# Gather buffers in borrowed memory, two expert steps behind every one-hot build

## The chip, the cores and the metric

The kernel runs on one core of one Trainium2 chip. The metric is the device time of one execution in microseconds.

## The reference

It is one inference step of a two-layer encoder over T = 576 frames (512 of a prompt and 64 of a running stream) of width 1024. Layer 0 mixes with a chunked gMLP, layer 1 with windowed attention. What matters here is the second half of each layer, a mixture of 16384 single-neuron experts:

```python
q = (xb @ w_q).reshape(blk, PEER_HEADS, 2, D_HALF)
sc = jnp.einsum('thpd,hpnd->thpn', q, sub_keys)
top_s, top_i = lax.top_k(sc, PEER_TOPK)                 # 8 heads, 2 halves, 16 of 128 keys
...
best_s, sel = lax.top_k(cand_s.reshape(...), PEER_TOPK)  # 16 of the 256 pairs
gate = jax.nn.softmax(best_s, axis=-1)
act = jax.nn.gelu(jnp.einsum('thkd,td->thk', exp_u[idx], xb))
return jnp.einsum('thk,thkd->td', gate * act, exp_v[idx])
```

Each frame picks 8 × 16 = 128 experts, each with a row of u and a row of v (2 × 1024 floats, 8 KB together).

## The kernel before

The frames are in two groups. Group d (256 frames, chunks 0 and 1) computes its experts densely on TensorE. Group g (320 frames, chunks 2, 3 and 4) gathers the rows that it needs.

**Dense part, per layer.** It goes over NPAIR = 64 pairs of expert columns. For each pair:

- SyncE loads 1 MB of u into `U[i % 2]` and 1 MB of v into `V[i % 2]`. The U load of pair i waits until the scores of pair i − 2 are done.
- TensorE computes `expert_scores(i)` (line 706) into bank i % 2, and ScalarE's `gelu(i)` (line 1059) writes it into a ring `gr` of RING = 16 entries.
- VectorE's `gate_product(i)` (line 1568) multiplies the ring entry by the gates in `Wr` and gives `a`.
- TensorE computes `expert_sums(i)` (line 719), which adds a × V.

The gates reach `Wr` through NBLD = 64 builds. VectorE's `one_hot(m)` (lines 1546 to 1557) makes one-hot tiles in two buffers, TensorE's `build(m)` (line 693) multiplies them, and ScalarE's `to_w(m)` (line 1051) copies the product out. one_hot(m) waits for build(m − 2). The gate product of pair 0 needs builds 0 to 15.

Each engine has its order written out by hand. On TensorE scores 0 to 6 come first (among the last selections); then, in what the text calls the hot stage, LEAD = 17 builds with scores 7 to 15 behind every second one; then a loop of sums(i), build(i + 17), score(i + 16); and from pair 48 on, sums alone.

**Gathered part, per layer.** It has NSTEP = 320 steps. In each, 128 partitions fetch one expert row of 8 KB: GpSimd issues an indirect DMA (`gather`, line 1259) into one of SLOTS = 6 slots, step s into slot s % 6, four of them in `gata` and two in `gatb`. VectorE forms a dot product with the frame (`dot_x`, line 1577), ScalarE a weight from it (lines 1065 and 1067), and VectorE adds weight × v row to `acc` (`axpy`, line 1585). `gathered(l, s)` is the dot of step s followed by the accumulation of step s − 1, and the gather into a slot waits for the accumulation that read it last (`ax_done`).

The table `AT` sets steps at places ahead of the pair loop: behind the adds of the output projection (`add`), the key searches (`top`), the selections (`sel`), attention units (`att`, layer 1), and behind each one_hot of the hot stage (`hot0` to `hot16`, two steps at every fourth place and one at the others). That makes EARLY = 47 steps in layer 0 and 52 in layer 1. The rest is spread evenly over the 64 pairs by `step0(l, i)`; of a pair's steps, HEAD = 2 come before gate_product(i + 1) and the rest after it.

SyncE also brings the saved h back (`hx`) near the end of the pairs, and loads the raw weight tiles of the next linear part. The first of these, `kvd`, go into `raw`, which shares its bytes with U.

Of the kernel before, what the change touches and what calls it, by code (L numbers as in the profile page):

```python
# [19 lines left out]
PH, TOPK, NK = 8, 16, 128  # L20
# [6 lines left out]
TD = 256  # L27
# [8 lines left out]
NBLD = (NK // CHUNK) * (TD // TB)  # L36
LEAD = PER + 1
RING, RING0 = 16, 8
RING_AT = 10
SLOTS = 6  # L40
NSTEP = 2 * P + DEC

TG_ = T - TD
# [2 lines left out]
CHUNKS = {"d": DC, "g": GC}  # L46
AT = (
    [("two", 4), ("mix", 1), *[(f"add{m}", 1) for m in range(6)], *[(f"top{m}", 1) for m in range(8, HP)],
     ("sel3", 3), ("sel4", 3), *[(f"hot{m}", 1 + (m % 4 == 0)) for m in range(LEAD)]],
    [*[(f"att{n}", 1) for n in range(1, 16, 2)], *[(f"add{m}", 1) for m in range(6)],  # L50
     *[(f"top{m}", 1) for m in range(8, HP)],
     ("sel2", 2), ("sel3", 3), ("sel4", 3), *[(f"hot{m}", 1 + (m % 4 == 0)) for m in range(LEAD)]])
EARLY = tuple(sum(n for _, n in a) for a in AT)
BEFORE_TOP = tuple(sum(n for p, n in a if p[:3] not in ("sel", "hot")) for a in AT)

# [98 lines left out]
def program(nc, xT, ckT, cv, gains, lin, uvd, uvg0, uvg1, skT, wsT, bs, sinks, dist, ident_c, iota_a, scaled_c, rank_c,  # L154
# [5 lines left out]
    with ExitStack() as ctx:  # L160
# [35 lines left out]
        i2 = at_("i2", 211040, [P, TD], F16)  # L196

        Wr = at_("Wr", 0, [P, PER, PER, 2, TB], F32)
        gr = at_("gr", 32768, [P, RING, 2 * TD], F32)
        hx = at_("hx", 53248, [P, DT, T], F32)  # L200
        oneA = at_("oneA", 65536, [P, 2, TB // TG, P, TG], F16)
        acc = at_("acc", 73728, [P, len(GC), D], F32)
        E = at_("E", 86016, [P, 2, CHUNK, TB], F16)
        B = at_("B", 88064, [P, 2, 2, CHUNK, TB], F16)
        gata = at_("gata", 92160, [P, 4, RD], F32)
        gatb = at_("gatb", 161792, [P, 2, RD], F32)
        idxg = at_("idxg", 124928, [P, NSTEP], U32)
# [28 lines left out]
        pT_ = {"g": at_("pT_g", 34816, [P, 2, 4, P], F32), "d": at_("pT_d", 87040, [P, 2, 4, P], F32)}  # L236
# [27 lines left out]
        bv, ex = (at_(n, 127488 + 512 * i, [P, PH, TOPK], F32) for i, n in enumerate(("bv", "ex")))  # L264
        gt = arena(TOPK, PH)
        bp = at_("bp", 128512, [P, PH, TOPK], U32)
# [28 lines left out]
        g_in = [sem(f"g_in{s}") for s in range(SLOTS)]  # L295
# [17 lines left out]

        def row(l, s):

            k = s % SLOTS
            return gata[:, k, :] if k < 4 else gatb[:, k - 4, :]

        def landed(l, s):

            k = s % SLOTS
            return g_in[k], 16 * (l * len(range(k, NSTEP, SLOTS)) + s // SLOTS + 1)

        def scored(i):

            return gr[:, (i + RING_AT) % RING, :]

        def gate_block(j, i):

# [41 lines left out]
        def wait_slot(eng, name, m):  # L371

            if m >= 4:
                last, k = name, m - 4
            elif name == "ing":
                return
            else:
                last = LOADS[LOADS.index(name) - 1]
                k = count(last) - 4 + m
            if last[-1] == "g":  # L380
                eng.wait_ge(lo_done[m % 4], LO[last] + k // 4 + 1)
            elif name == "kvd":
# [32 lines left out]
        def _(sp):  # L415
# [12 lines left out]
            def experts(l):  # L428
# [25 lines left out]
                for i in range(NPAIR - 2):  # L454
                    sp.wait_ge(sums_done, i + NPAIR * l + 1)
                    v_load(i + 2, i % 2)
                    if i + RING + 2 < NPAIR:
                        next_u(i + RING + 2)
                    if i == NPAIR - RING_AT - 1:
                        sp.wait_ge(a_done, NPAIR * l + NPAIR - RING_AT)  # L460
                        sp.wait_ge(full[3], BASE[f"bld{l}"][3] + NBLD // 2)
                        sp.dma_start(hx[:, :, :].rearrange("p a t -> p (a t)"), hsp).then_inc(h_in, 16)
                for s in range(2):
# [21 lines left out]
        def _(pe):  # L485
# [240 lines left out]
            def experts(l):  # L726
# [12 lines left out]
                    expert_scores(l, i, i % 2)  # L739
                for m in range(LEAD):  # L740
                    build(l, m, m % 2)
                    if m % 2 == 0:
                        expert_scores(l, RING0 - 1 + m // 2, (RING0 - 1 + m // 2) % 2)
                for i in range(2):
                    expert_sums(l, i, i, first=i == 0)
                    build(l, i + LEAD, (i + LEAD) % 2)
# [142 lines left out]
        def _(act):  # L889
# [180 lines left out]
            def experts(l):  # L1070
                n = 0
                for i in range(2 if l else 3, NTC):
                    gelu(l, n)
                    gate_exp(l, i)
                    gelu(l, n + 1)
                    weights_at(l, f"sel{i}")
                    n += 2
                for c in DC:
                    gates_high(l, c)
                gelu(l, n)  # L1080
                weights_at(l, "hot0")
                for i in range(n + 1, RING0 - 1):
                    gelu(l, i)
                for m in range(1, LEAD):
                    weights_at(l, f"hot{m}")
                    to_w(l, m - 1)
                    if m % 2 == 1:
                        gelu(l, RING0 - 1 + m // 2)
# [145 lines left out]
        def _(pool):  # L1234
# [581 lines left out]
```

## Time and profile before

| what | value |
|---|---|
| median of three runs | 3287.66 us (3287.6 to 3296.01) |
| profiled execution | 3287.6 us, span 3285.8 us |
| TensorE matmuls busy | 2960.6 us, 90% |
| VectorE busy | 2474.0 us, 75% |
| GpSimd busy | 1139.2 us, 35% |
| ScalarE busy | 806.0 us, 25% |
| moved by DMA | 1042.99 MB, mean 317 GB/s |

How to read the rows: a row of a timeline has the start in us from the span's start, the length in us, the engine, the line and the operation, output<-inputs, the shape and a count. An idle time before it and what ended it stand in square brackets. A row may merge several instructions, and the ends of matmuls are modelled and overlap the next row a little, so periods are taken from start to start. A row of the windows gives the stretch, its length, the busy us (and count) of PE, PEld, DVE, ACT and POOL, then the granted TensorE clock (1.00 is full), the busy share of the DMA engines and GB/s. PE is TensorE, PEld its weight load, DVE VectorE, ACT ScalarE, POOL GpSimd, SP SyncE.

### The profile page before, as it was taken

To read this page: it belongs to the slowest core of one execution; us is meant where nothing else is said; L and a number is where in the kernel's file an instruction comes from. 1 tells how busy PE (TensorE), PEld (TensorE's weight loads), DVE (VectorE), ACT (ScalarE), POOL (GpSimd) and SP (SyncE) were. 2 spreads that over 40 slices of the span, in tenths; PEclk is the share of its full clock that TensorE was granted. 3 is DMA by queue.
4 is the path that set the end of the run, shared out by engine and by line. 5 is a ranking of instruction groups with operands and counts; after the bars stand their busy time and mean duration, and the time that the engine had idled before them with its cause. 6 is when DMAs were issued, how large, how long until landed. Compare 5 with 4: busy or idle time off the path is not lost.

```text
span 3285.8 us, 46700 instructions
## 1 busy us (share of the span) xinstructions
PE 2960.6 (90%) x17310; PEld 2589.3 (79%) x17310; DVE 2474.0 (75%) x5433; ACT 806.0 (25%) x2386; POOL 1139.2 (35%) x840
## 2 busy tenths in 40 slices
PE   6899979999999999966778978789999999999856
PEld 5787868888888888855666857679888888888744
DVE  4276797888887888778643776898788778887778
ACT  3332222211111111111344353222111121111112
POOL 4542022333333333444354420122333333333432
PEclk9999989999999999988877978889999999999887
DMA  4336668999999999999521356678999999999996
GB/s 155 98 99 219 240 250 308 356 413 410 411 410 419 412 412 412 407 422 421 202 69 46 102 180 240 224 272 315 407 409 409 407 406 406 410 406 409 413 420 271
DMA packets 159967, 1042.99 MB, mean 317 GB/s; under 512 B 18480, under 2 KB 23920, under 8 KB 44096
## 3 DMA queue, kind: packets, MB, share of 16 engines
q0 software_dynamic: 92160, 671.13, 50.7%
q1 hardware_dynamic: 63648, 357.59, 28.0%
q10 hardware_dynamic: 4000, 12.36, 1.1%
q8 instruction: 74, 1.21, 0.1%
q14 instruction: 85, 0.70, 0.1%
HBM read 1033.28 MB, written 7.86 MB: 317 GB/s over the span
## 4 chain that ended last, share of the span: by engine, by line
PE 78%; DMA 10%; DVE 6%; issue 4%; ACT 1%; POOL 1%; SPq 0%; DVEq 0%; ACTq 0%; POOLq 0%
PE bank L706 28%; PE bank L719 20%; PE bank L693 8%; PE bank L510 7%; DMA gata<-uvg,idxg 7%; PE bank L497 3%; PE bank L498 3%; PE bank L499 3%; DMA gatb<-uvg,idxg 2%; DVE acc L1585 2%; PE bank L595 1%; PE bank L527 1%; PE bank L851 1%; DVE rstd L1341 1%; PE bank L829 1%
## 5 line engine op out<-in xcount | busy, mean ns | idle before, releaser
L719 PE MATMUL bank<-a,V 128*128 128x256 f32 x4096 | 950.4, 393 | 120.0 <-DVE a L1568 112.1
L719 PEld LDWEIGHTS bank<-a,V 128*128 128x128 f32 x4096 | 808.9, 198 | 245.5 <-issue 120.7
L1259 POOL DMA_INDIRECT gata<-uvg,idxg x428 | 578.5, 1352 | 1204.1 <-DVE acc L1585 1148.3
L706 PE MATMUL bank<-xd,U 128*128 128x256 f32 x4096 | 933.7, 387 | 0.9 <-DMA U<-uvd 0.8
L706 PEld LDWEIGHTS bank<-xd,U 128*128 128x128 f32 x4096 | 787.0, 195 | 105.5 <-DMA U<-uvd 1.4
L1585 DVE SCALAR_TENSOR_TENSOR acc<-gata,wgt,acc 128x1024 f32<-128x1024 f32 x428 | 547.7, 1280 | 203.6 <-ACT wgt L1067 203.4
L1577 DVE CUSTOM_DVE_ANT_0 gata<-gata,xrow 128x1024 f32<-128x1024 f32 x428 | 520.6, 1217 | 57.1 <-DMA gata<-uvg,idxg 55.3
L1259 POOL DMA_INDIRECT gatb<-uvg,idxg x212 | 284.0, 1339 | 563.0 <-DVE acc L1585 551.6
L1065 ACT ACTIVATE act<-dot 128x1 f32<-128x1 f32 x640 | 127.1, 199 | 1071.2 <-DVE dot L1577 1071.1
L1585 DVE SCALAR_TENSOR_TENSOR acc<-gatb,wgt,acc 128x1024 f32<-128x1024 f32 x212 | 271.4, 1280 | 103.0 <-ACT wgt L1067 103.0
L693 PEld LDWEIGHTS bank<-B,oneA 128*128 128x128 f16 x4096 | 281.0, 150 | 11.3 <-issue 0.6
L693 PE MATMUL bank<-B,oneA 128*128 128x32 f16 x4096 | 283.0, 247 | 0.2 <-issue 0.2
L1577 DVE CUSTOM_DVE_ANT_0 gatb<-gatb,xrow 128x1024 f32<-128x1024 f32 x212 | 257.9, 1216 | 21.3 <-DMA gatb<-uvg,idxg 19.9
L1059 ACT ACTIVATE gr<-bank 128x512 f32<-128x512 f32 x128 | 76.5, 597 | 734.9 <-PE bank L706 734.9
L510 PE MATMUL bank<-xd,raw 128*128 128x256 f32 x1088 | 249.5, 387 | 7.5 <-DVE xd L1348 7.1
L510 PEld LDWEIGHTS bank<-xd,raw 128*128 128x128 f32 x1088 | 208.5, 194 | 36.7 <-issue 9.0
L497 PE MATMUL bank<-xh,wh 128*128 128x320 f32 x608 | 201.0, 331 | 32.7 <-POOL xl L404 24.2
L1067 ACT ACTIVATE wgt<-act,gateg 128x1 f32<-128x1 f32 x640 | 188.7, 295 | 20.8
L498 PE MATMUL bank<-xl,wh 128*128 128x320 f32 x608 | 192.1, 316 | 0.0
L499 PE MATMUL bank<-xh,wl 128*128 128x320 f32 x608 | 192.0, 316 | 0.0
L1551 DVE TENSOR_TENSOR oneA<-iotaA,i 128x1024 f16<-128x1024 f16 x256 | 169.1, 700 | 0.0
L1297 POOL TENSOR_TENSOR wl<-raw,wh 128x1024 fp32r<-128x1024 f32 x48 | 116.3, 2426 | 116.5 <-ACT wh L905 116.5
(193 smaller groups left out, 2575.3 us busy)
## 6 DMA issues: line engine op xcount, KB each, us to landing
U<-uvd SPq DMA_DIRECT2D x128, 1024.0 KB, 8.8
V<-uvd SPq DMA_DIRECT2D x128, 1024.0 KB, 9.0
raw<-lin SPq DMA_DIRECT2D x152, 512.0 KB, 3.6
gata<-uvg,idxg POOLq DMA_INDIRECT x428, 9.9
hsp<-h ACTq DMA_DIRECT2D x2, 2304.0 KB, 13.9
hx<-hsp SPq DMA_DIRECT2D x2, 2304.0 KB, 16.6
gatb<-uvg,idxg POOLq DMA_INDIRECT x212, 10.1
sk_g<-skT ACTq DMA_DIRECT2D x2, 1024.0 KB, 4.8
```

Of the source, the lines that this page charges most:

```text
L497: pe.matmul(out, whi, xh[:, k, :], start=(k == 0), stop=False)
L498: pe.matmul(out, whi, xl[:, k, :], start=False, stop=False)
L499: mm = pe.matmul(out, wlo, xh[:, k, :], start=False, stop=(k == DT - 1))
L510: mm = pe.matmul(bank[s][:, 0:TD], raw[:, s, P * k:P * k + P], x[:, k, :], start=(k == 0), stop=(k == DT - 1))
L693: mm = pe.matmul(bank[2 + s][:, CHUNK * t:CHUNK * (t + 1)], oneA[:, s, t // TG, :, t % TG], B[:, s, part, :, t], start=(t == 0 and part == ...
L706: mm = pe.matmul(bank[s][:, TD * t:TD * t + TD], U[:, s, o:o + P], xd[:, k, :], start=(t == 0 and k == 0), stop=(k == DT - 1), skip_group_ ...
L719: mm = pe.matmul(bank[b][:, TD * (d % 2):TD * (d % 2) + TD], V[:, s, o:o + P], a[:, s, TD * k:TD * k + TD], start=(first and k == 0 and d ...
L1067: act.activation(wgt[:, k:k + 1], act8[:, k:k + 1], ACT.Copy, scale=gateg[:, s:s + 1])\
L1259: pool.indirect_dma_start(row(l, s), None, uvg[l], bass.IndirectOffsetOnAxis(idxg[:, s:s + 1], 0)).then_inc(g_in[s % SLOTS], 16)
L1551: ins = dve.tensor_tensor(oneA[:, s, u], iotaA[:, :, :], i1[:, None, t + TG * u:t + TG * u + TG].broadcast_to([P, P, TG]), ALU.is_equal)
L1577: dve.tensor_tensor_reduce(u, u, xrow[:, min(s // P, 2), :], 1.0, 0.0, ALU.mult, ALU.add, dot[:, s % 8:s % 8 + 1]).then_inc(dot_done, 1)
L1585: dve.scalar_tensor_tensor(out=acc[:, n, :], in0=row(l, s)[:, D:RD], scalar=wgt[:, s % 8:s % 8 + 1], in1=acc[:, n, :], op0=ALU.mult, op1=A ...
```

## The change

- **Gather slots.** Step s no longer goes to slot s % 6. A table `SLOT`, made by `slots(l)`, picks the free slot that was used longest ago. Four slots (`gat`) are always free to use. Two more (`gatb`, now at another address) may be used from step `early(l, "hot0").stop + 4` up to step `late` = step0(l, 48) + 2. From `late` up to step 311 the two U buffers are used in their place, once the last scores (pairs 62 and 63) have read them. The last eight steps have the four slots alone.
- **Ring.** `gr` is split into `gra` (entries 0 to 7, where gatb was) and `grb` (entries 8 to 15), and pair i uses entry i % 16; before it was (i + 10) % 16.
- **Places.** Every `hot` place has two steps (34 instead of 22), so EARLY is 59 and 64.
- **Order in the hot stage.** Scores 7 to 15 follow builds 0 to 8, one each, and builds 9 to 16 stand without scores. ScalarE's gelus follow.
- **Waits.** The hx load moves from pair 53 to pair 50 of SyncE's order and waits for the last step that used gatb. The kvd loads wait also until 312 steps are accumulated (`ax_done` of NSTEP − 8). GpSimd no longer waits for all steps before its first low parts of kvg.
- **Addresses.** hx, pT_d, bv, ex and bp lie elsewhere.

```diff
-RING_AT = 10
-SLOTS = 6
+SLOTS = 4
-     ("sel3", 3), ("sel4", 3), *[(f"hot{m}", 1 + (m % 4 == 0)) for m in range(LEAD)]],
+     ("sel3", 3), ("sel4", 3), *[(f"hot{m}", 2) for m in range(LEAD)]],
...
-            k = s % SLOTS
-            return gata[:, k, :] if k < 4 else gatb[:, k - 4, :]
+            k = SLOT[l][s][0]
+            return gat[:, k, :] if k < SLOTS else U[:, k - SLOTS, :] if k < SLOTS + 2 else gatb[:, k - SLOTS - 2, :]
...
+        def slots(l):
+            late, last = step0(l, NPAIR - RING) + 2, NSTEP - 8
+            hot = early(l, "hot0").stop + SLOTS
+            used, table = [-1] * (SLOTS + 4), []
+            for s in range(NSTEP):
+                free_ = [*range(SLOTS), *((SLOTS + 2, SLOTS + 3) if hot <= s < late else ()),
+                         *((SLOTS, SLOTS + 1) if late <= s < last else ())]
+                k = min(free_, key=lambda j: (used[j], j))
+                table.append((k, used[k]))
+                used[k] = s
+            return table
...
             elif name == "kvd":
                 for b in range(2):
                     eng.wait_ge(full[b], BASE["peer0"][b] + NPAIR // 2)
+                eng.wait_ge(ax_done, NSTEP - 8)
...
-                    if i == NPAIR - RING_AT - 1:
-                        sp.wait_ge(a_done, NPAIR * l + NPAIR - RING_AT)
+                    if i == NPAIR - RING + 2:
+                        sp.wait_ge(ax_done, NSTEP * l + max(s for s in range(NSTEP) if SLOT[l][s][0] >= SLOTS + 2) + 1)
...
                     build(l, m, m % 2)
-                    if m % 2 == 0:
-                        expert_scores(l, RING0 - 1 + m // 2, (RING0 - 1 + m // 2) % 2)
+                    if RING0 - 1 + m < RING:
+                        expert_scores(l, RING0 - 1 + m, (m + 1) % 2)
...
-                if s >= SLOTS:
-                    pool.wait_ge(ax_done, NSTEP * l + s - SLOTS + 1)
+                k, last = SLOT[l][s]
+                if last >= 0:
+                    pool.wait_ge(ax_done, NSTEP * l + last + 1)
+                elif k >= SLOTS + 2:
+                    pool.wait_ge(ax_done, NSTEP * l + early(l, "hot0").stop)
+                elif k >= SLOTS:
+                    b = k - SLOTS
+                    pool.wait_ge(full[b], BASE[f"peer{l}"][b] + NPAIR // 2)
...
-                if name == "kvg":
-                    pool.wait_ge(ax_done, NSTEP)
```

## Rows read from the trace of the kernel before

**Rows 1.** The page's part 4: the chain that ended last, by engine.

```profile
PE 78%; DMA 10%; DVE 6%; issue 4%; ACT 1%; POOL 1%; SPq 0%; DVEq 0%; ACTq 0%; POOLq 0%
```

**Rows 2.** Windows of layer 0's expert part: hot stage, pair loop, tail.

```profile
555.00:621.00 66.00, 66.00 (x507) 59.54 (x506) 59.40 (x100) 15.81 (x46) 19.40 (x15) 0.92 0.82 303
700.00:1384.00 684.00, 684.00 (x4102) 612.02 (x4101) 550.96 (x797) 131.28 (x452) 255.52 (x183) 1.00 1.00 412
1520.00:1560.00 40.00, 27.14 (x96) 22.00 (x95) 32.69 (x42) 6.47 (x26) 16.73 (x13) 0.80 1.01 421
```

**Rows 3.** TensorE's timeline, hot stage of layer 0: start, length, what.

```profile
518.52 7.17 PE L706 MATMUL bank<-xd,U 128*128 128x256 f32 x32 [0.79 <-DMA U<-uvd]
...
577.40 7.14 PE L706 MATMUL bank<-xd,U 128*128 128x256 f32 x32
584.38 4.29 PE L693 MATMUL bank<-B,oneA 128*128 128x32 f16 x64
588.48 8.83 PE L706 MATMUL bank<-xd,U 128*128 128x256 f32 x32
597.15 4.30 PE L693 MATMUL bank<-B,oneA 128*128 128x32 f16 x64
...
621.02 7.07 PE L719 MATMUL bank<-a,V 128*128 128x256 f32 x32
```

**Rows 4.** VectorE's timeline, hot stage of layer 0.

```profile
575.55 0.43 DVE L1546 TENSOR_TENSOR E<-iotaA,i 128x512 f16<-128x512 f16 x1 [3.10 <-PE bank L693]
...
580.11 0.42 DVE L1546 TENSOR_TENSOR E<-iotaA,i 128x512 f16<-128x512 f16 x1
...
587.00 0.42 DVE L1546 TENSOR_TENSOR E<-iotaA,i 128x512 f16<-128x512 f16 x1
...
618.76 0.68 DVE L1568 TENSOR_TENSOR a<-gr,Wr 128x512 f32<-128x512 f32 x1
```

**Rows 5.** TensorE's timeline, selection and hot stage of layer 1.

```profile
2118.90 0.28 PE L643 MATMUL bank<-W 64*64 64x128 f16 x1 [18.55 <-issue]
...
2120.71 9.30 PE L706 MATMUL bank<-xd,U 128*128 128x256 f32 x32
...
2189.72 7.14 PE L706 MATMUL bank<-xd,U 128*128 128x256 f32 x32
...
2293.83 7.07 PE L719 MATMUL bank<-a,V 128*128 128x256 f32 x32
```

**Rows 6.** The dot products of line 1577 between 290 and 1377.5 us.

```profile
L1577 DVE DVE_READ_ACCUMULATOR2_ANT dot<- x253: 71/79/86, 304.6 to 1375.7; 128x1 f32 x127
```

**Rows 7.** The gathers of line 1259 up to 1384 us, from issue to landing.

```profile
DMA to landing us min/median/max: 5.2/9.7/18.9
```

**Rows 8.** GpSimd's timeline, end of layer 0's scores.

```profile
1367.10 1.68 POOL L1259 DMA_INDIRECT gata<-uvg,idxg  x1 [4.85 <-DVE acc L1585]
...
1380.27 1.68 POOL L1259 DMA_INDIRECT gata<-uvg,idxg  x1 [1.80 <-DVE acc L1585]
```

**Rows 9.** TensorE's timeline, end of layer 0's scores.

```profile
1376.66 7.07 PE L706 MATMUL bank<-xd,U 128*128 128x256 f32 x32
1383.57 13.98 PE L719 MATMUL bank<-a,V 128*128 128x256 f32 x64
```

**Rows 10.** Transfers of layer 0's tail, 1390 to 1590 us.

```profile
DMA packets 11488, 82.87 MB, mean 414 GB/s; under 512 B 1280, under 2 KB 1280, under 8 KB 1792
...
raw<-lin SPq DMA_DIRECT2D x4, 512.0 KB, 17.6
```

**Rows 11.** VectorE's timeline, last steps of layer 0.

```profile
1583.73 1.23 DVE L1577 CUSTOM_DVE_ANT_0 gatb<-gatb,xrow 128x1024 f32<-128x1024 f32 x1
...
1586.22 1.23 DVE L1577 CUSTOM_DVE_ANT_0 gata<-gata,xrow 128x1024 f32<-128x1024 f32 x1
```

**Rows 12.** GpSimd's timeline, early steps of layer 0.

```profile
336.93 0.94 POOL L1259 DMA_INDIRECT gatb<-uvg,idxg  x1 [9.37 <-DVE acc L1585]
```

**Rows 13.** VectorE's timeline, early steps of layer 0.

```profile
345.02 1.22 DVE L1577 CUSTOM_DVE_ANT_0 gata<-gata,xrow 128x1024 f32<-128x1024 f32 x1
```

More of the change, by code:

```diff
@@ L48 @@
     [("two", 4), ("mix", 1), *[(f"add{m}", 1) for m in range(6)], *[(f"top{m}", 1) for m in range(8, HP)],
-     ("sel3", 3), ("sel4", 3), *[(f"hot{m}", 1 + (m % 4 == 0)) for m in range(LEAD)]],
+     ("sel3", 3), ("sel4", 3), *[(f"hot{m}", 2) for m in range(LEAD)]],
     [*[(f"att{n}", 1) for n in range(1, 16, 2)], *[(f"add{m}", 1) for m in range(6)],
      *[(f"top{m}", 1) for m in range(8, HP)],
-     ("sel2", 2), ("sel3", 3), ("sel4", 3), *[(f"hot{m}", 1 + (m % 4 == 0)) for m in range(LEAD)]])
+     ("sel2", 2), ("sel3", 3), ("sel4", 3), *[(f"hot{m}", 2) for m in range(LEAD)]])
 EARLY = tuple(sum(n for _, n in a) for a in AT)
@@ L198, in program @@
         Wr = at_("Wr", 0, [P, PER, PER, 2, TB], F32)
-        gr = at_("gr", 32768, [P, RING, 2 * TD], F32)
-        hx = at_("hx", 53248, [P, DT, T], F32)
+        grb = at_("grb", 32768, [P, RING - RING0, 2 * TD], F32)
+        gatb = at_("gatb", 49152, [P, 2, RD], F32)
+        hx = at_("hx", 49152, [P, DT, T], F32)
         oneA = at_("oneA", 65536, [P, 2, TB // TG, P, TG], F16)
@@ L204, in program @@
         B = at_("B", 88064, [P, 2, 2, CHUNK, TB], F16)
-        gata = at_("gata", 92160, [P, 4, RD], F32)
-        gatb = at_("gatb", 161792, [P, 2, RD], F32)
+        gat = at_("gat", 92160, [P, SLOTS, RD], F32)
         idxg = at_("idxg", 124928, [P, NSTEP], U32)
@@ L210, in program @@
         V = at_("V", 145408, [P, 2, RD], F32)
+        gra = at_("gra", 161792, [P, RING0, 2 * TD], F32)
         a = at_("a", 198656, [P, 2, 2 * TD], F32)
@@ L235, in program @@
         S_ = {"g": at_("S_g", 28672, [P, SS, 2, 2 * P], F32), "d": at_("S_d", 153600, [P, SS, 2, 2 * P], F32)}
-        pT_ = {"g": at_("pT_g", 34816, [P, 2, 4, P], F32), "d": at_("pT_d", 87040, [P, 2, 4, P], F32)}
+        pT_ = {"g": at_("pT_g", 34816, [P, 2, 4, P], F32), "d": at_("pT_d", 161792, [P, 2, 4, P], F32)}
         ck = at_("ck", 38912, [P, 2, P], F32)
@@ L263, in program @@
         cand, cr = arena(PH, NC), arena(PH, NC)
-        bv, ex = (at_(n, 127488 + 512 * i, [P, PH, TOPK], F32) for i, n in enumerate(("bv", "ex")))
+        bv, ex = (arena(PH, TOPK) for _ in range(2))
         gt = arena(TOPK, PH)
-        bp = at_("bp", 128512, [P, PH, TOPK], U32)
+        bp = arena(PH, TOPK, dt=U32)
         bph, rank2 = (arena(PH * TOPK // 2).bitcast(F16).rearrange("p (k q) -> p k q", q=PH) for _ in range(2))
@@ L294, in program @@
         u_in, v_in = [sem(f"u_in{s}") for s in range(2)], [sem(f"v_in{s}") for s in range(2)]
-        g_in = [sem(f"g_in{s}") for s in range(SLOTS)]
+        g_in = [sem(f"g_in{s}") for s in range(SLOTS + 4)]
         gsel_done = sem("gsel_done")
@@ L314, in row @@
         def row(l, s):
-            k = s % SLOTS
-            return gata[:, k, :] if k < 4 else gatb[:, k - 4, :]
+            k = SLOT[l][s][0]
+            return gat[:, k, :] if k < SLOTS else U[:, k - SLOTS, :] if k < SLOTS + 2 else gatb[:, k - SLOTS - 2, :]
         def landed(l, s):
-            k = s % SLOTS
-            return g_in[k], 16 * (l * len(range(k, NSTEP, SLOTS)) + s // SLOTS + 1)
+            k = SLOT[l][s][0]
+            return g_in[k], 16 * (l * FILLS[0][k] + sum(j == k for j, _ in SLOT[l][:s + 1]))
         def scored(i):
-            return gr[:, (i + RING_AT) % RING, :]
+            k = i % RING
+            return gra[:, k, :] if k < RING0 else grb[:, k - RING0, :]
         def gate_block(j, i):
@@ L339, in early @@
             return range(0)
+        def slots(l):
[9 more added lines that the diff above has]
+            return table
+        SLOT = [slots(l) for l in range(2)]
+        FILLS = [[sum(k == j for k, _ in SLOT[l]) for j in range(SLOTS + 4)] for l in range(2)]
         def steps(l, i):
@@ L1086, in experts @@
                     to_w(l, m - 1)
-                    if m % 2 == 1:
-                        gelu(l, RING0 - 1 + m // 2)
+                    if RING0 + m - 2 < RING - 1:
+                        gelu(l, RING0 + m - 2)
                 for i in range(NPAIR):
@@ L1255, in gather @@
             def gather(l, s):
-                if s >= SLOTS:
-                    pool.wait_ge(ax_done, NSTEP * l + s - SLOTS + 1)
+                k, last = SLOT[l][s]
[6 more added lines that the diff above has]
+                    pool.wait_ge(full[b], BASE[f"peer{l}"][b] + NPAIR // 2)
                 pool.indirect_dma_start(row(l, s), None, uvg[l],
-                                        bass.IndirectOffsetOnAxis(idxg[:, s:s + 1], 0)).then_inc(g_in[s % SLOTS], 16)
+                                        bass.IndirectOffsetOnAxis(idxg[:, s:s + 1], 0)).then_inc(g_in[k], 16)
             def experts(l):
```

## The prediction

> **What bounds the kernel now.** I read the chain of waits first. It puts 78% of the span on TensorE and 10% on transfers [rows 1], so I then asked for busy time by stage of the expert part [rows 2]. In layer 0 three stages follow each other. In the hot stage (17 one-hot builds, seven to fifteen expert scores) TensorE is busy for all 66.0 us of the stretch shown and VectorE for 59.4. In the pair loop TensorE is busy for 684.0 of 684.0 us at full clock, while the transfers run at 412 GB/s. In the last sixteen pairs, which I call the tail, TensorE is busy for 27.1 of 40 us, and the transfers run at 421 GB/s. So the hot stage and the loop are set by TensorE and the tail by bytes. A step here is one gathered expert row per token: a gather of 1 MB, a dot product and an accumulation.
>
> **The hot stage, the largest term.** Before, a place of one step takes VectorE 580.11 − 575.55 = 4.56 us and a place of two steps 587.00 − 580.11 = 6.89 us, one-hot included [rows 4]. The change makes all 17 places two-step places: 12 steps more, 12 × 2.33 = 28 us of VectorE work. What of it shows depends on TensorE's order. Before, scores and builds alternate one to two, and TensorE is full until its first sums at 621.02 [rows 3]. After, scores 7 to 15 follow builds 0 to 8 one by one, and builds 9 to 16 come alone.
>
> While scores last, TensorE has a build (half of 588.48 − 584.38 = 2.05 us) and a score (584.38 − 577.40 = 6.98) for each place, 9.03 us, more than VectorE's 6.89, so the extra steps are covered. Every second score before took 597.15 − 588.48 = 8.67 us, each time behind two builds. In the loop one build stands ahead of a score and the clock is full [rows 2], so I take 6.98 for all nine. Score 7 starts at 518.52 and ends at 525.5; eight times 9.03 later, at 597.7, score 15 ends, and build 9 at 599.8. one_hot(11) waits for exactly that build, because the one-hot buffers are two deep. From there the cover is gone: six places (11 to 16) × 6.89 = 41.3 us, then the gate product, 0.68 [rows 4], and sums(0) starts at 641.8. That is 20.8 us after 621.02. Layer 1 in the same way: 2189.72 + 6.98 + 72.2 + 2.05 + 41.3 + 0.7 = 2313.0 against 2293.83 [rows 5], 19.2 us later. Bounds for each layer: 18 us, if the place is slightly shorter, and 31 us, if five of the nine scores still take 8.67 (+8.5) and VectorE's place grows by the tail's pace of 2.49 us for a step [rows 11] (+1.7).
>
> TensorE then comes out of 40 us in which it is busy for 2 of each 6.9 us. The nearest row is a score behind an idle time of 18.55 us: 9.30 us [rows 5] against 6.98, so +2.3 for each layer (bounds 0 and 3.1). The Trainium skill (TensorE: Matmul & The Clock Gate, "What's actually happening") says that the engine's slow clock of 1.2 GHz is the default and only activity lifts it; the trace agrees with its 9.30. Without that charge the sum would be 4.6 lower.
>
> **The loop.** There are 12 steps fewer after the hot stage (261 instead of 273 in layer 0, 256 instead of 268 in layer 1), spread over 64 pairs. Three quarters of them leave the loop, where TensorE sets the pace: 0. The depth of gathers is six there as before, with the two borrowed buffers in another place. This costs nothing either.
>
> **The tail.** Step 253 is the first one behind gate_product(49), since 253 dots stand before 1377.5 [rows 6]. After, the step at this place has number 256, so 64 steps instead of 67 are left: 3 × 1.05 MB / 421 GB/s = −7.5 us. In layer 0 the four raw tiles of kvd (2.1 MB) also land in the tail before [rows 10]; they will now wait until 312 steps are accumulated, which gives −5.0. They are needed only after the norm, so their delay is covered by the last steps.
>
> Against this stands a new wait. From that step on, two gathers go to the U buffers, and the second can't be issued before score 63 has ended at 1383.6 [rows 9]. It stands at the head of GpSimd's queue, so all gathers behind it are held. Before, five had been issued by then (1367.10 to 1380.27 [rows 8]), and with some 10 us to landing about 3.5 MB of them had landed or were under way: +8.3 us. Filling an empty queue again: +2. Bounds of the two together: 0 and 17 (the whole of 1383.6 − 1367.1).
>
> The last eight steps have four slots. A slot's turn is the landing, then two dots and two accumulations (2 × 2.49 = 5.0 us [rows 11]). Landing takes 5.2 us at the least and 9.7 in the median [rows 7]; with few in flight I take 8. (5.0 + 8) / 4 = 3.25 against 2.49, but only the steps whose slot is late pay it: half of 8 × 0.76, +3 (bounds 0 and 6). The Trainium skill (DMA: Bandwidth & Descriptors, "Anatomy of one DMA — SWDGE (gpsimd) path") gives 2.0 us plus the bytes at 436 GB/s, an estimate of 4.4 us for 1 MB, with which the ring would cost nothing and the sum would be 6 lower. The trace's minimum of 5.2 lies above it. Tail: layer 0 −7.5 − 5.0 + 8.3 + 2 + 3 = +0.8; layer 1, without kvd, +5.8.
>
> **The early steps.** Four slots instead of six serve the steps ahead of the hot stage. The tightest place is the six adds, one each 3.5 to 3.9 us. Step 8's gather would go out at 336.93, when step 4 is accumulated, and is wanted at 345.02 [rows 12, 13]: 8.1 us, about what a landing takes. I take 1 us for each layer (bounds 0 and 4). Bursts of three in sel3 and sel4 lie some 20 us apart, and the stall that VectorE could get at hot places 1 and 2 lies beside TensorE's scores. hx is loaded three pairs earlier with the same bytes: 0. The other moves of buffers change addresses only: 0.
>
> **Sum.** 20.8 + 19.2 + 4.6 + 0.8 + 5.8 + 2 = 53.2. The profiled execution took 3287.6 us (span 3285.8), the same as the median of 3287.66 within 0.1. So 3341 us, 1.6% slower.
>
> **Rivals.**
> - *Gathers are short of slots.* The held gathers cost their full 17 us (+6.7 in each layer), the ring of four its 6 (+3), the early steps their 4 (+3), and the hot stage 4 more through VectorE waiting for rows: +33, 3374. For it: the tail already waits on gathers. Against it: bytes, not latency, fill the tail [rows 2].
> - *The tail catches up.* Five gathers issued at once fill the transfers, and the held bytes cost nothing: −13.3 in each layer, 3315. Against it: 421 GB/s is already there for all of the tail [rows 2] and leaves little to catch up with.
> - *Faster: the loop is limited by bytes.* Nine gathers fewer in each loop would then give 9 × 1.05 / 0.412 = 23 us each, and with the tail of the last rival the end is 3341 − 46 − 27 = 3268. It decides if TensorE waits for U or V anywhere in the loop; it is busy 684.0 of 684.0.
> - *No change.* The VectorE work after score 15 stays hidden. TensorE would need 42 us of its own work there; it has seven builds, 14 us. About 3290.
>
> **How the numbers follow.** Main case 0.64, with a range of its own of 3325 to 3358; short of slots 0.15; tail catches up 0.14; faster 0.03; no change 0.04. The range 3312 to 3370 leaves out the last two, most of the first rival's upper half and the end of the second. A measurement of this kernel tells about 0.3% from no change. Faster 0.03, same 0.04, slower 0.93.
>
> **What would show it.** In the changed profile: all nine scores of the hot stage near 7 us with single builds between; then seven builds alone, 6.9 us apart, with TensorE idle and VectorE full; sums(0) 41 to 43 us after build 9; the loop at 15.9 us for each pair; a gap of 14 to 17 us in GpSimd's gathers where the scores end; and a tail as long as before within 8 us. I am wrong if sums(0) follows score 15 within 25 us, if the loop's period moves, or if the tail changes by more than 15 us.

## The result, and the profile after

The changed kernel took 3344.63 us (median of four runs, 3338.97 to 3348.8), the kernel before 3291.84 us in the runs beside it. The ratio is 1.016 with an interval of 1.0133 to 1.0185. The forecast was 3341 us in a range of 3312 to 3370. The profiled execution took 3343.85 us, with a span of 3342.0, 56.2 us more than the 3285.8 before.

I read the new profile in the order of the prediction's steps. First TensorE's timeline in the hot stage of layer 0, from the ninth build on. It answers to [rows 3]. Line 724 is the expert scores, 711 the builds and 737 the sums.

```profile
588.36 2.23 PE L711 MATMUL bank<-B,oneA 128*128 128x32 f16 x32
590.40 7.14 PE L724 MATMUL bank<-xd,U 128*128 128x256 f32 x32
597.38 4.30 PE L711 MATMUL bank<-B,oneA 128*128 128x32 f16 x64
602.07 2.25 PE L711 MATMUL bank<-B,oneA 128*128 128x32 f16 x32 [0.38 <-issue]
609.01 2.26 PE L711 MATMUL bank<-B,oneA 128*128 128x32 f16 x32 [4.69 <-DVE B L1579]
615.96 2.25 PE L711 MATMUL bank<-B,oneA 128*128 128x32 f16 x32 [4.70 <-DVE B L1579]
...
636.81 2.22 PE L711 MATMUL bank<-B,oneA 128*128 128x32 f16 x32 [4.69 <-DVE B L1579]
642.17 9.47 PE L737 MATMUL bank<-a,V 128*128 128x256 f32 x32 [3.14 <-issue]
651.47 2.23 PE L711 MATMUL bank<-B,oneA 128*128 128x32 f16 x32
653.52 7.14 PE L724 MATMUL bank<-xd,U 128*128 128x256 f32 x32
```

Score 15 starts at 590.40 and takes 6.98 us (to the next row). Then come builds alone: 9 and 10 at once, and from build 12 on one each 6.95 us, behind 4.7 us of idle time that VectorE's B tiles end. The first sums start at 642.17, against 621.02 before, and the forecast said 641.8. These sums take 651.47 − 642.17 = 9.30 us, where later ones take 6.9.

The windows of the same kernel (columns as in [rows 2]) show the lone builds and the loop:

```profile
602.00:642.00 40.00, 13.47 (x192) 12.70 (x192) 40.00 (x63) 8.88 (x30) 15.04 (x12) 0.51 0.87 310
720.00:1407.00 687.00, 687.00 (x4117) 614.07 (x4116) 533.11 (x774) 128.13 (x435) 235.93 (x171) 1.00 0.98 396
```

VectorE is busy for 40.00 of 40 us, and TensorE for 13.5 at a clock of 0.51. In the loop TensorE is busy for 687.0 of 687.0 us as before, while the transfers have fallen from 412 to 396 GB/s.

Now GpSimd's gathers where the scores end. They answer to [rows 8]:

```profile
1382.54 1.68 POOL L1283 DMA_INDIRECT gat<-uvg,idxg  x1 [0.66 <-DVE acc L1607]
1394.26 0.94 POOL L1283 DMA_INDIRECT U<-uvg,idxg  x1 [10.04 <-PE bank L724]
1407.57 0.94 POOL L1283 DMA_INDIRECT U<-uvg,idxg  x1 [12.38 <-PE bank L724]
1408.81 0.93 POOL L1283 DMA_INDIRECT gat<-uvg,idxg  x1 [0.30 <-issue]
1410.05 0.94 POOL L1283 DMA_INDIRECT gat<-uvg,idxg  x1 [0.30 <-issue]
```

The first gather into U waited 10.04 us for TensorE's scores and the second 12.38 us. Between 1382.54 and 1407.57, 25 us, only one gather left, and then five went out within 6 us. VectorE's last eight steps in layer 0 answer to [rows 11], and the raw tiles of kvd to [rows 10]:

```profile
1607.13 1.23 DVE L1599 CUSTOM_DVE_ANT_0 gat<-gat,xrow 128x1024 f32<-128x1024 f32 x1 [4.43 <-DMA gat<-uvg,idxg]
...
1616.26 1.22 DVE L1599 CUSTOM_DVE_ANT_0 gat<-gat,xrow 128x1024 f32<-128x1024 f32 x1 [1.67 <-DMA gat<-uvg,idxg]
```

```profile
raw<-lin SPq DMA_DIRECT2D x4, 512.0 KB, 7.8
```

VectorE waited 4.43 and 1.67 us for rows there. The four raw tiles were issued from 1594.68 to 1596.06 and took 6.2 to 11.8 us, so all of them landed by 1608, ahead of the last of these steps at 1616.26.

To compare all kernels I cut each profiled span by the same marks in each layer: the first build, the first sums, the last matmul of the scores and the last accumulation, all as start times. For the changed kernel's layer 0 they stand in these rows (first and last start), one from each of three lines:

```profile
L737 PE MATMUL bank<-a,V x2048: 378/379/767, 642.2 to 1603.8; 128*128 128x256 f32 x187
```

```profile
L724 PE MATMUL bank<-xd,U x2048: 378/379/742, 431.5 to 1406.9; 128*128 128x256 f32 x187
```

```profile
L1607 DVE SCALAR_TENSOR_TENSOR acc<-gat,wgt,acc x224: 1270/1279/1404, 304.7 to 1618.8; 128x1024 f32<-128x1024 f32 x112
```

The hot stage is then first build to first sums, the loop first sums to last score, and the tail last score to last accumulation. Times in us, layer 0 / layer 1:

| kernel | hot stage | loop | tail | span |
|---|---|---|---|---|
| before | 105.5 / 106.1 | 762.4 / 762.6 | 207.8 / 199.2 | 3285.8 |
| changed | 127.6 / 126.1 | 764.7 / 765.3 | 211.9 / 205.7 | 3342.0 |
| e1_places | 115.4 / 120.6 | 762.5 / 762.6 | 201.6 / 192.8 | 3300.9 |
| e2_order | 116.7 / 116.6 | 764.6 / 765.0 | 211.3 / 199.2 | 3318.5 |
| e3_both | 126.7 / 126.1 | 765.1 / 765.3 | 200.5 / 192.7 | 3318.1 |
| e4_slots_places | 115.9 / 125.8 | 762.3 / 762.6 | 211.2 / 206.8 | 3328.1 |
| e5_slots | 105.6 / 106.3 | 762.4 / 762.4 | 221.1 / 213.6 | 3307.5 |
| e6_six_to_end | 126.6 / 126.0 | 764.8 / 765.4 | 205.4 / 200.8 | 3331.5 |
| e7_late8 | 126.9 / 126.0 | 764.6 / 765.6 | 199.5 / 195.7 | 3319.1 |
| e8_loop_rate | 115.2 / 122.6 | 762.4 / 762.6 | 179.1 / 162.3 | 3244.5 |
| e9_rate_only | 103.1 / 106.2 | 762.6 / 762.4 | 200.9 / 181.0 | 3264.3 |
| e10_rate_438 | 115.3 / 122.7 | 762.5 / 762.6 | 170.8 / 152.9 | 3229.0 |
| e11_rate_450 | 113.5 / 120.2 | 771.6 / 772.6 | 163.4 / 145.9 | 3229.9 |

The stages repeat better than whole spans, within some 2.5 us where the code of the stage is the same. What lies ahead of layer 0's first build scatters more: it starts between 514.6 and 522.7 in the kernels with six slots and between 511.8 and 520.2 in those with four. What lies between the layers scatters by some 5 us. Each row is one profiled execution.

### The profile page after: what moved, and what is told of

Same layout as the page of the kernel before. It is cut to its first block, busy times and chain, and to the rows that moved or that the text cites. A ratio compares the mean times of both kernels' runs of the same rounds, so it can differ in the third digit from the quotient of the medians.

```text
span 3342.0 us, 46699 instructions
## 1 busy us (share of the span) xinstructions
PE 2962.7 (89%) x17310; PEld 2588.0 (77%) x17310; DVE 2474.3 (74%) x5433; ACT 807.7 (24%) x2386; POOL 1114.4 (33%) x840
## 4 chain that ended last, share of the span: by engine, by line
PE 75%; DMA 10%; DVE 7%; issue 5%; ACT 1%; POOL 1%; SPq 0%; DVEq 0%; ACTq 0%; POOLq 0%
PE bank L724 27%; PE bank L737 20%; DMA gat<-uvg,idxg 8%; PE bank L528 7%; PE bank L711 7%; PE bank L515 3%; PE bank L517 3%; PE bank L516 3%; DVE acc L1607 2%; DMA U<-uvg,idxg 1%; PE bank L613 1%; PE bank L545 1%; PE bank L869 1%; PE bank L847 1%; DVE rstd L1363 1%
## 5 line engine op out<-in xcount | busy, mean ns | idle before, releaser
L737 PE MATMUL bank<-a,V 128*128 128x256 f32 x4096 | 961.8, 396 | 119.8 <-DVE a L1590 107.7
L1283 POOL DMA_INDIRECT gat<-uvg,idxg x452 | 589.3, 1304 | 1392.2 <-DVE acc L1607 1324.8
L724 PE MATMUL bank<-xd,U 128*128 128x256 f32 x4096 | 920.7, 383 | 1.4 <-DMA U<-uvd 1.4
L724 PEld LDWEIGHTS bank<-xd,U 128*128 128x128 f32 x4096 | 777.1, 192 | 102.8 <-DMA U<-uvd 1.8
L1607 DVE SCALAR_TENSOR_TENSOR acc<-gat,wgt,acc 128x1024 f32<-128x1024 f32 x452 | 578.1, 1279 | 230.8 <-ACT wgt L1085 230.6
L1599 DVE CUSTOM_DVE_ANT_0 gat<-gat,xrow 128x1024 f32<-128x1024 f32 x452 | 549.4, 1216 | 89.1 <-DMA gat<-uvg,idxg 86.6
L1283 POOL DMA_INDIRECT gatb<-uvg,idxg x150 | 202.1, 1347 | 372.2 <-DVE acc L1607 370.7
L1607 DVE SCALAR_TENSOR_TENSOR acc<-gatb,wgt,acc 128x1024 f32<-128x1024 f32 x150 | 191.6, 1277 | 106.7 <-ACT wgt L1085 106.6
L528 PEld LDWEIGHTS bank<-xd,raw 128*128 128x128 f32 x1088 | 207.6, 194 | 36.7 <-issue 9.0
L516 PE MATMUL bank<-xl,wh 128*128 128x320 f32 x608 | 192.7, 317 | 0.0
L1599 DVE CUSTOM_DVE_ANT_0 gatb<-gatb,xrow 128x1024 f32<-128x1024 f32 x150 | 182.0, 1213 | 5.3 <-DMA gatb<-uvg,idxg 5.3
L515 PEld LDWEIGHTS bank<-xh,wh 128*128 128x128 f32 x608 | 118.5, 195 | 44.7 <-issue 32.8
## 6 DMA issues: line engine op xcount, KB each, us to landing
hsp<-h ACTq DMA_DIRECT2D x2, 2304.0 KB, 12.4
```

What stands on the lines that cost most here:

```text
L515: pe.matmul(out, whi, xh[:, k, :], start=(k == 0), stop=False)
L516: pe.matmul(out, whi, xl[:, k, :], start=False, stop=False)
L528: mm = pe.matmul(bank[s][:, 0:TD], raw[:, s, P * k:P * k + P], x[:, k, :], start=(k == 0), stop=(k == DT - 1))
L724: mm = pe.matmul(bank[s][:, TD * t:TD * t + TD], U[:, s, o:o + P], xd[:, k, :], start=(t == 0 and k == 0), stop=(k == DT - 1), skip_group_ ...
L737: mm = pe.matmul(bank[b][:, TD * (d % 2):TD * (d % 2) + TD], V[:, s, o:o + P], a[:, s, TD * k:TD * k + TD], start=(first and k == 0 and d ...
L1283: pool.indirect_dma_start(row(l, s), None, uvg[l], bass.IndirectOffsetOnAxis(idxg[:, s:s + 1], 0)).then_inc(g_in[k], 16)
```

## The experiments

### One part at a time

The change has three parts: the steps at the hot places, the order of scores and builds, and the slots. Four kernels take them apart.

**e1_places** is the kernel before with the new places alone.

```diff
-*[(f"hot{m}", 1 + (m % 4 == 0)) for m in range(LEAD)]
+*[(f"hot{m}", 2) for m in range(LEAD)]
```

> The kernel before with two steps at every hot place, its order of scores and builds and its six slots kept. Theory (the extra steps show only because the new order takes the scores from behind the builds): TensorE's own work still fills the hot stage. VectorE starts one_hot(2) at 517.8 and needs 15 places of 6.89 us, so sums(0) of layer 0 starts at 621.8 to 627 (621.0 before); in layer 1 17 places from 2185.3 on give 2303, +9. The tail has three gathers fewer, -7.5 in each layer. Sum about 3287 (3278 to 3296). Rival (28 us of VectorE work in each layer must show in any order): sums(0) 20 us later in each layer, 3312.

Measured: 3302.74 us, 1.0041 of before (1.0024 to 1.0057), 7 us over my range. The hot stages grew by 9.9 and 14.5 us, the tails fell by 6.2 and 6.4. Both ideas of the hot stage were off: mine by 4 to 9 us in layer 0 and by 5.5 in layer 1, the rival's by 10 and 5.5 the other way. VectorE's timeline in layer 0 comes first:

```profile
515.82 1.28 DVE L1585 SCALAR_TENSOR_TENSOR acc<-gata,wgt,acc 128x1024 f32<-128x1024 f32 x1 [5.19 <-ACT wgt L1067]
...
525.32 1.28 DVE L1585 SCALAR_TENSOR_TENSOR acc<-gatb,wgt,acc 128x1024 f32<-128x1024 f32 x1 [2.46 <-ACT wgt L1067]
...
623.89 0.69 DVE L1568 TENSOR_TENSOR a<-gr,Wr 128x512 f32<-128x512 f32 x1
```

VectorE waited 5.19 and 2.46 us for weights at the first places. ScalarE forms them in its order, and there they stand behind a gelu that waits for TensorE's score. The first of these waits costs nothing: the one_hot behind it starts at 517.02, against 517.76 before. From 526 us on VectorE is full. It ends the first gate product at 624.6, inside my forecast of 621.8 to 627 for the sums. TensorE waits for VectorE here and there, and its own last rows hold the rest:

```profile
577.62 2.24 PE L693 MATMUL bank<-B,oneA 128*128 128x32 f16 x32 [2.65 <-DVE B L1557]
579.68 9.58 PE L706 MATMUL bank<-xd,U 128*128 128x256 f32 x32
589.10 2.23 PE L693 MATMUL bank<-B,oneA 128*128 128x32 f16 x32
...
621.38 8.83 PE L706 MATMUL bank<-xd,U 128*128 128x256 f32 x32
630.04 7.07 PE L719 MATMUL bank<-a,V 128*128 128x256 f32 x32
```

What I had left out is score 15. In the old order it stands behind build 16 and ahead of the first sums. Build 16 needs the last one_hot, and VectorE has only the two steps of the last place to do beside this score. It starts at 621.38 and takes 630.04 − 621.38 = 8.66 us, so the sums follow the end of the gate product by 5.5 us. In layer 1 it is the same, by 5.1 us, and there that is nearly the whole miss of 5.5:

```profile
2308.24 0.69 DVE L1568 TENSOR_TENSOR a<-gr,Wr 128x512 f32<-128x512 f32 x1
```

```profile
2305.75 8.43 PE L706 MATMUL bank<-xd,U 128*128 128x256 f32 x32
2314.02 7.07 PE L719 MATMUL bank<-a,V 128*128 128x256 f32 x32
```

The scores were also slower than I took them: the build at 577.62 waited 2.65 us, and the score behind it took 589.10 − 579.68 = 9.42 us instead of 6.98. Only the last one of them shows. So with the old order the 28 us of VectorE work show by a third in layer 0 and by half in layer 1.

**e2_order** is the kernel before with the new order alone, on TensorE and on ScalarE.

```diff
-                    if m % 2 == 0:
-                        expert_scores(l, RING0 - 1 + m // 2, (RING0 - 1 + m // 2) % 2)
+                    if RING0 - 1 + m < RING:
+                        expert_scores(l, RING0 - 1 + m, (m + 1) % 2)
...
-                    if m % 2 == 1:
-                        gelu(l, RING0 - 1 + m // 2)
+                    if RING0 + m - 2 < RING - 1:
+                        gelu(l, RING0 + m - 2)
```

> The kernel before with the new order alone (scores 7 to 15 behind builds 0 to 8), one or two steps at the hot places as before, six slots. Theory: places 11 to 16 take four times 4.56 and two times 6.89 us, 32.0 us, instead of 41.3, so sums(0) comes 11 us late in each layer, and the first sums are 2.4 us longer for the slow clock. No tail term. Sum 3287.6 + 27 = 3315 (3308 to 3320). Rival (the order alone is neutral, only the extra steps cost): 3288.

Measured: 3320.96 us, 1.0093 (1.0065 to 1.012), 1 us over my range. Hot stages +11.2 and +10.5, loops +2.2 and +2.4, layer 1's tail unchanged. Layer 0's tail is 3.5 us longer, which the edit doesn't explain; differences of layer 0's tail between single profiles may be off by that much. The order alone has a price, with no step added: it takes TensorE's scores away from the places where VectorE is the slower one.

**e3_both** has both edits on the kernel before.

> The kernel before with the new order and two steps at every hot place, six slots in their old places. Theory: the hot stage as in the changed kernel (+21, +20, +5 for the clock), the tail three gathers shorter (-7.5 in each layer) with none held back: 3318 (3312 to 3324). What is left to the changed kernel's 3344 is the price of the slots, 26 us. Rival (slots cost nothing beyond the hot stage): 3340 or more, and the tail as long as in the changed kernel.

Measured: 3328.01 us, 1.0119 (1.0098 to 1.014), 4 us over my range. The profiled execution took 3319.93 us (span 3318.1) and is the fastest of the four; no profile shows where the others spent 7 to 10 us more. Hot stages +21.2 and +20.0, loops +2.7 each, tails −7.3 and −6.5. The hot stages and loops are those of the changed kernel within 1 us. Against e2_order the extra steps add 10.0 and 9.5 us to the hot stages. What is left to the changed kernel, 11.4 us in layer 0's tail and 13.0 in layer 1's, is the price of the slots. The two ratios to the kernel before differ by 0.0041, which is 13 us, and their intervals allow some 10 us either way.

**e4_slots_places** is the changed kernel with the old order (the diff of e2_order backwards).

> The changed kernel with the old order of scores and builds. Theory: the hot stage as in e1_places (+1 to +6 in layer 0, +9 in layer 1), the tail as in the changed kernel (+4.0 and +6.5 by its trace): 3311 (3302 to 3318). Rival (VectorE's steps show in any order): 3335 or more.

Measured: 3326.35 us, 1.0111 (1.009 to 1.0132), 8 us over my range. The tails are the changed kernel's within 1.1 us. The hot stages grew by 10.4 and 19.7 instead of 1 to 6 and 9. Most of that is the miss of e1_places again, score 15 behind build 16; the rest is in layer 1, for the most part on VectorE's timeline:

```profile
2207.15 0.42 DVE L1568 TENSOR_TENSOR E<-iotaA,i 128x512 f16<-128x512 f16 x1
...
2213.71 1.23 DVE L1599 CUSTOM_DVE_ANT_0 gat<-gat,xrow 128x1024 f32<-128x1024 f32 x1 [1.92 <-DMA gat<-uvg,idxg]
...
2216.06 0.42 DVE L1568 TENSOR_TENSOR E<-iotaA,i 128x512 f16<-128x512 f16 x1
...
2221.60 1.23 DVE L1599 CUSTOM_DVE_ANT_0 gat<-gat,xrow 128x1024 f32<-128x1024 f32 x1 [0.91 <-DMA gat<-uvg,idxg]
```

With four slots the rows of hot places 1 and 2 land late, 1.92 and 0.91 us. VectorE is the bound here, so this shows. In the changed kernel the same waits (1.93 and 1.96 us) lie beside TensorE's scores.

### The slots

**e5_slots** is the changed kernel with the old order and the old places, so its slots, ring and waits alone.

> The changed kernel with the old order and the old hot places, so its slots, ring and waits alone. Theory: nothing in the hot stage; the tail as much longer as the changed kernel's is against e3_both's (11.4 us in layer 0, 13.0 in layer 1), so tails of 219 and 212 us and a time of 3312 (3305 to 3318). Rival (the slots cost only together with the extra steps): tails of 208 and 199 us, 3288.

Measured: 3313.4 us, 1.007 (1.0044 to 1.0097). The hot stages are those of before within 0.2 us, the tails 13.3 and 14.4 us longer. The slots cost this much by themselves, with nothing else changed in the hot stage.

**e6_six_to_end** keeps the U buffers in use to the last step of the changed kernel.

```diff
-            late, last = step0(l, NPAIR - RING) + 2, NSTEP - 8
+            late, last = step0(l, NPAIR - RING) + 2, NSTEP
...
-                eng.wait_ge(ax_done, NSTEP - 8)
+                eng.wait_ge(ax_done, NSTEP)
```

> The changed kernel with the two U buffers in use up to the last step, and kvd waiting for the last accumulation. Theory: the ring of four at the end costs 3 us in each layer, up to 6, so tails of 206 to 209 and 200 to 203 us instead of 211.9 and 205.7, about 3336. Rival (the last steps are paced by bytes, not slots): tails unchanged, 3343.

Measured: 3334.08 us, 1.0133 (1.011 to 1.0156). The tails are 6.5 and 4.9 us shorter than the changed kernel's. The ring of four at the end cost about that, so the last steps are not paced by bytes alone. In layer 0 the figure includes the raw tiles of kvd, which now load behind the last accumulation.

**e7_late8** lets gathers go to gatb for six steps more before U takes over.

```diff
-            late, last = step0(l, NPAIR - RING) + 2, NSTEP - 8
+            late, last = step0(l, NPAIR - RING) + 8, NSTEP - 8
...
-                    if i == NPAIR - RING + 2:
+                    if i == NPAIR - RING + 4:
```

> The changed kernel with the step from which U buffers take gathers moved from step0(l, 48) + 2 to + 8, and hx two pairs later, so that no gather stands before TensorE's last scores. Theory: the gap in GpSimd's gathers at the end of the scores is gone and the tails are 10 us shorter, 202 and 196 us, 3323. Rival (the held bytes are caught up): gap gone, tails unchanged, 3343.

Measured: 3322.41 us, 1.0098 (1.0075 to 1.0121). GpSimd's timeline where the scores end (they end at 1411.05):

```profile
1404.72 1.23 POOL L1283 DMA_INDIRECT gatb<-uvg,idxg  x1 [0.67 <-DVE acc L1607]
1407.74 1.68 POOL L1283 DMA_INDIRECT gat<-uvg,idxg  x1 [1.80 <-DVE acc L1607]
1409.72 0.94 POOL L1283 DMA_INDIRECT U<-uvg,idxg  x1 [0.31 <-issue]
1411.48 0.94 POOL L1283 DMA_INDIRECT U<-uvg,idxg  x1 [0.82 <-PE bank L724]
```

The wait for scores is down to 0.82 us. The windows of 60 us around the last score, first the changed kernel and then this one, give 326 GB/s and 407 GB/s:

```profile
1377.00:1437.00 60.00, 52.97 (x259) 45.92 (x257) 36.59 (x46) 9.80 (x36) 15.69 (x14) 0.96 0.82 326
```

```profile
1381.00:1441.00 60.00, 57.11 (x280) 49.82 (x279) 47.79 (x61) 11.67 (x44) 27.02 (x19) 0.97 0.99 407
```

The pause held back (407 − 326) GB/s × 60 us = 4.9 MB, which is 11.5 us at 421 GB/s. The tails are 12.4 and 10.0 us shorter. The held bytes were not caught up.

### Where the moved gathers should leave from

The change moves twelve steps of each layer ahead of the pair loop, but only three of them leave the tail, because `step0` spreads the rest evenly. The next kernels keep the slots and the order of before and change how the steps are spread.

**e8_loop_rate** is e1_places with this:

```diff
         def step0(l, i):
-            return EARLY[l] + i * (NSTEP - EARLY[l]) // NPAIR
+            if i <= NPAIR - RING:
+                return EARLY[l] + i * 17 // 4
+            s = EARLY[l] + (NPAIR - RING) * 17 // 4
+            return s + (i - NPAIR + RING) * (NSTEP - s) // RING
```

> e1_places with 4.25 steps for each of the first 48 pairs, so the twelve steps taken by the hot stage all leave the tail (55 and 50 gathers left there instead of 67 and 65). Theory (the tail is set by bytes, the loop by TensorE): hot stage +10 and +14.5 as in e1_places, tails -30 and -37: 178 and 162 us, 3245. Rival (the tail is set by TensorE or by latency once bytes are fewer): tails of 190 us, 3270.

Measured: 3250.98 us, 0.9884 of before (0.9864 to 0.9904). The tails fell by 28.7 and 36.9 us, and the hot stages grew by 9.7 and 16.5. The same edit of the hot places that cost 0.4% in e1_places gains 1.2% when the steps come off the tail. In layer 0 these are the twelve steps that were moved. In layer 1 fifteen leave the tail, because the loop takes three more than before. The forecast of the tails was right within 1.1 us. The time is 6 us over the 3245 that I named.

**e9_rate_only** is the kernel before with 35 // 8 in the place of 17 // 4 and the old places.

> The kernel before, its hot places and order kept, with 4.375 steps for each of the first 48 pairs (61 and 56 gathers left in the tail instead of 67 and 65). Theory: the loop still keeps TensorE's 15.9 us for each pair, since 6.375 x 1.05 MB in it is 420 GB/s, just under the 421 of the tail; tails -15 and -22 us, hot stages unchanged: 3250 (3245 to 3262). Rival (the loop turns into one set by bytes at this rate, as the rival that the loop is limited by bytes would have it): loops of 775 us or more instead of 762.4, 3275.

Measured: 3266.57 us, 0.9926 (0.99 to 0.9952), 5 us over my range. Loops of 762.6 and 762.4, tails −6.9 and −18.2 instead of −15 and −22. TensorE isn't held up, but the loop's window is at 419 GB/s, and VectorE now waits for rows there, which it did not before:

```profile
700.00:1380.00 680.00, 680.00 (x4083) 607.40 (x4082) 564.14 (x805) 134.17 (x457) 220.30 (x186) 1.00 1.01 419
```

```profile
DVE gata L1580 <- DMA gata<-uvg,idxg: 62.2, 57, 3.2
DVE gatb L1580 <- DMA gatb<-uvg,idxg: 25.4, 25, 2.9
```

It waited 62.2 + 25.4 us. Some of the missing gain is work that is behind when the loop ends. The dot products begun up to layer 0's last score, first in the kernel before and then in this one:

```profile
L1577 DVE DVE_READ_ACCUMULATOR2_ANT dot<- x255: 71/79/86, 304.6 to 1381.1; 128x1 f32 x128
```

```profile
L1580 DVE DVE_READ_ACCUMULATOR2_ANT dot<- x259: 74/81/93, 311.7 to 1386.6; 128x1 f32 x130
```

These are four more, where the table of steps moves six ahead of that place. Two steps at 2.49 us are 5.0 of the 8.1 us that layer 0 misses. In layer 1 there are eight more instead of nine (265 against 257), 2.5 of 3.8 us. The rest stays open.

**e10_rate_438** is e8_loop_rate with 35 // 8.

> e8_loop_rate with 4.375 instead of 4.25 steps for each of the first 48 pairs (49 and 44 gathers left). Theory: six gathers fewer in each tail than in e8_loop_rate, -15 us each, loops of 762.5 us: tails of 164 and 147 us, 3221 (3214 to 3232). Rival (the loop is set by bytes at this rate): loops of 775 us or more, no gain over 3251.

Measured: 3232.72 us, 0.9826 (0.9805 to 0.9847), just over my range. Loops unchanged, tails 170.8 and 152.9: another 8 to 9 us each, where 15 were forecast. Again four of six steps were done ahead of layer 0's last score (271 dot products against 267 in e8_loop_rate), and 4 × 2.49 us is 10.

**e11_rate_450** is e8_loop_rate with 9 // 2.

> e8_loop_rate with 4.5 steps for each of the first 48 pairs (43 and 38 gathers left). Theory: 6.5 x 1.05 MB at 421 GB/s is 16.2 us for a pair, so the loop turns from TensorE's pace to that of bytes, 774 to 780 us; tails -30 us against e8_loop_rate, 149 and 132 us: about 3217, no better than e10_rate_438. Rival (TensorE alone paces the loop, whatever the bytes): loops of 762.5, 3191.

Measured: 3235.33 us, 0.9831 (0.9803 to 0.9859), 18 us over the forecast. The loops take 771.6 and 772.6, the only kernel in which they grow without the order's slow first sums. The tails fall by only 7.4 and 7.0 against e10_rate_438, so the two balance. The windows of e10_rate_438 and e11_rate_450:

```profile
700.00:1380.00 680.00, 680.00 (x4105) 607.63 (x4104) 565.91 (x807) 134.95 (x458) 223.68 (x186) 1.00 1.01 420
```

```profile
700.00:1380.00 680.00, 677.29 (x4059) 602.41 (x4058) 564.43 (x808) 132.88 (x454) 212.60 (x186) 0.99 1.01 419
```

TensorE is busy for 680.0 of 680 us in the first and for 677.3 in the second, both at 419 to 420 GB/s. What TensorE waits for are not U or V but VectorE's one-hot tiles, and VectorE waited 76.3 + 36.7 us for gathered rows in the same window:

```profile
PE bank L696 <- DVE B L1560: 2.7, 5, 1.2
```

So the loop slows down by way of VectorE. That bytes are what makes the rows late is argued from the transfers, which stay at 419 to 420 GB/s when more gathers are asked for; a kernel with more than six slots was not run. e10_rate_438 and e11_rate_450 can't be told apart by their times, and both are 1.7% faster than before.

## Why the prediction was right

The change is slower by the main case's mechanism and nearly by its sum: 56.2 us of span against 53.2. That the sum is this close is partly luck: the tails came out 4.0 us above the forecast in all and the early steps 3.5 below, and what lies ahead of the first build scatters by 8 us from profile to profile. Term by term:

| term | forecast | measured |
|---|---|---|
| first sums, layer 0 | 641.8 | 642.17 |
| hot stage of layer 1 | +19.2 | +20.0 |
| slow clock behind the lone builds | +2.3 / +2.3 | +2.3 / +2.7 (loops) |
| loop otherwise | 0 | 0 |
| tail, layer 0 | +0.8 | +4.1 |
| tail, layer 1 | +5.8 | +6.5 |
| early steps | +2 | −0.9 and −0.6 |

The layer 0 hot stage is +22.1, from a first build that started 0.9 us earlier; the forecast was 20.8. 22.1 + 20.0 + 2.3 + 2.7 + 4.1 + 6.5 − 0.9 − 0.6 = 56.2.

**Hot stage.** The timeline shows the nine scores at 6.98 us with single builds, then builds alone, and VectorE full beside them. e2_order and e3_both show that the order opens the gap: alone it costs 11 us in each layer, and the extra steps add 10 once it is open. The place of two steps was 6.95 instead of 6.89. I did not foresee that the extra steps would also show in the old order (e1_places), so "the extra steps are covered while scores last" is right for the new order and was wrong when I carried it over to the old one, where the last score stands behind the last build.

**Clock.** The price was right in layer 0 and a little low in layer 1, where the first sums took 9.92 us. The Trainium skill (TensorE: Matmul & The Clock Gate, "What's actually happening") has the slow clock as the default that activity lifts. The traces agree: the granted clock was 0.51 in the window of lone builds, half of full and so the 1.2 GHz level, and still 0.51 from 642 to 647 us, in the first half of the sums that took 9.30 us.

**Tail.** Its parts were less exact than their sum. Three gathers fewer gave −6.2 to −7.3 (e1_places and e3_both), not −7.5. The held gathers and the refill, forecast at 10.3, are worth 12.4 and 10.0 (e7_late8). The ring of four, forecast at 3, is worth 6.5 and 4.9 (e6_six_to_end, the first figure with kvd in it), near its upper bound of 6.

The pause was not the one that I described. I counted only the wait of the second gather into U and named a gap of 14 to 17 us. The first one also stands for a score, 10.04 us, and the gap was 25 us with one gather in it. 4.9 MB were held back in layer 0, not 3.5.

The kvd relief of −5.0 is the step that was argued worst. The four raw tiles went out at step 312 and all landed in the tail, so their bytes did not leave it; at most they used time that the ring of four left free. The relief was not measured by itself. If the ring costs the same in both layers, the tiles still cost 6.5 − 4.9 = 1.6 us, and the relief is an estimated 3.4. The parts add up for the slots alone: in layer 1 10.0 + 4.9 = 14.9 against 14.4 in e5_slots, in layer 0 12.4 + 6.5 − 5.0 = 13.9 against 13.3 (the 6.5 holds what the tiles still cost, so their whole 5.0 comes off). In the changed kernel they cost 1.9 and 2.5 us less than these sums (13.0 and 11.4), and that stays open.

**Loop.** Nine gathers fewer changed nothing: 412 GB/s fell to 396 and TensorE's pace stayed. So the rival in which bytes limit the loop falls for this change. e11_rate_450 shows where the loop begins to suffer, above 4.375 steps for a pair, and that it does so through VectorE's late rows.

**Early steps.** Nothing shows beyond the scatter of the stages ahead. Up to 505 us VectorE waited for no gathered row in either kernel, and ahead of layer 1's hot stage for 1.5 us before and 1.7 us after, so four slots cost next to nothing there. The waits of 1.93 and 1.96 us at hot places 1 and 2 of layer 1 are covered, as forecast.

**The rivals.** "The tail catches up" falls with e7_late8. "Gathers are short of slots" was right in its direction (the ring) and too large elsewhere. "No change" needed cover behind score 15, and VectorE's 40.00 of 40 us leaves none.

## What to carry to other kernels

Before moving work from one stage to another, ask which stage each moved piece leaves. Twelve gathers went into a stage in which they cost 10 to 20 us, and nine of them left one where they had cost nothing. With all of them taken from the stage that bytes limit, the same edit of the hot places gained 1.2%, and 1.7% with the loop filled close to its own limit. An order of two kinds of work is worth keeping mixed where one covers another engine's time: all scores first leaves builds with nothing beside them. Look also at what stands last: a score behind the last build is hardly covered once the other engine is the slower one (5 us in e1_places; the order without it was not run). A borrowed buffer that is free a few us too late holds everything behind it in its queue; let the old buffer serve until the new one is free.

## What the runs showed of the hardware

- TensorE at its own pace and the transfers at 419 to 420 GB/s fit beside each other (e10_rate_438, loops of 762.5 us). VectorE's waits for rows grow first, from none before to 62.2 + 25.4 us in e9_rate_only, before TensorE loses anything.
- A score behind a build that had waited 2.65 us took 9.42 us instead of 6.98, at a granted clock of 0.77 over 580 to 590 us (e1_places). A slow score also comes without idle time: in the kernel before, one straight behind two builds took 8.67 us, at 0.83 over 588 to 598 us.
- Gathers held for 25 us and then issued 1.24 us apart (1407.57 to 1408.81) brought the transfers to 425 GB/s in the 40 us from 1420 on, against 422 in the same window before. That is 0.1 MB more, and 4.9 MB had been held, so next to nothing of the pause came back.
